# Four modulation rows to a PSUM bank: one copy and one turn where there were four

## What is computed

```
def adaln(cond, mod_w, mod_b):
    return jnp.split(jax.nn.silu(cond) @ mod_w + mod_b, 6, axis=-1)

for l in range(DEPTH):
    sh_a, sc_a, g_a, sh_f, sc_f, g_f = [m[:, None, :] for m in adaln(c, mod_w[l], mod_b[l])]
    csh_a, csc_a, cg_a, csh_f, csc_f, cg_f = adaln(c_ctx, mod_w[l], mod_b[l])
    hx = modulate(rms_norm(x, norm_mix_g[l]), sh_a, sc_a)
    ...
    x = x + g_a * (y_x @ w_out[l])
    x = x + g_f * swiglu(modulate(rms_norm(x, norm_ffn_g[l]), sh_f, sc_f), ffn_w_in[l], ffn_w_out[l])
```

## Time and profile before

| | |
|---|---|
| median of three executions | 2587.45 us (2583.33 to 2587.89) |
| the profiled execution's own time | 2582.74 us |
| its span, first to last instruction | 2581.0 us |
| TensorE matmuls busy | 2403.8 us, 93% of the span |
| VectorE busy | 1536.8 us, 60% |
| ScalarE busy | 1014.6 us, 39% |
| matmuls of the turns (L697) | 192 records, from 20.6 to 657.2 us |
| matmuls of modulation chunks (L714) | 384 records, 51.9 us |
| copies of rows (L1169) | 24, of 573 to 599 ns |
| mean granted TensorE clock | 0.966 of full speed |

### The profile page before, as it was taken

The page is one execution under the profiler, slowest core; times in us unless marked ns, Lnnn a source line. Parts: engine busy times, 40 slices in busy tenths (PEclk is TensorE's granted clock), DMA queues, the critical chain, the costliest instruction groups (busy, mean ns, idle before and its releaser), DMA issues.

```text
span 2581.0 us, 33638 instructions
## 1 busy us (share of the span) xinstructions
PE 2403.8 (93%) x14430; PEld 2063.1 (80%) x14430; DVE 1536.8 (60%) x1957; ACT 1014.6 (39%) x1214; POOL 0.2 (0%) x4
## 2 busy tenths in 40 slices
PE   5978989999989899899899998999998999999997
PEld 3765667777768767899878876899987978779997
DVE  3777553233346566655667668574667657766565
ACT  4245542121233134434554343343465434334344
POOL 0000000000000000000000000000000000000000
PEclk8989999999999999999999999999999999999999
DMA  7440133444323231445445453445544545344552
GB/s 290 165 175 1 52 145 148 184 169 167 114 98 114 72 76 46 151 180 196 167 177 183 147 190 129 163 180 181 183 172 157 190 147 198 126 175 157 187 182 98
DMA packets 61115, 389.22 MB, mean 151 GB/s; under 512 B 6568, under 2 KB 11048, under 8 KB 15784
## 3 DMA queue, kind: packets, MB, share of 16 engines
q1 hardware_dynamic: 60968, 387.08, 41.6%
HBM read 386.00 MB, written 1.05 MB: 150 GB/s over the span
## 4 chain that ended last, share of the span: by engine, by line
PE 76%; DVE 15%; ACT 5%; issue 3%; DMA 1%; SPq 0%; DVEq 0%; ACTq 0%
PE PS L468 22%; PE PS L469 21%; PE PS L470 21%; DVE w_lo L1432 4%; PE PS L641 2%; PE PS L672 2%; PE PS L714 2%; DVE BIG L1939 2%; ACT w_hi L1042 1%; PE PS L654 1%; PE PS L602 1%; PE PS L858 1%; PE PS L840 1%; PE PS L697 1%; ACT xn L1120 1%
## 5 line engine op out<-in xcount | busy, mean ns | idle before, releaser
L1432 DVE TENSOR_TENSOR w_lo<-raw,w_hi 128x2048 fp32r<-128x2048 f32 x300 | 682.6, 2290 | 568.8 <-ACT w_hi L1042 566.5
L1042 ACT ACTIVATE w_hi<-raw 128x2048 fp32r<-128x2048 f32 x300 | 571.4, 1911 | 765.3 <-PE PS L470 468.2
L468 PE MATMUL PS<-x_hi,w_hi 128*128 128x256 f32 (+1 forms) x2048 | 634.2, 310 | 29.1 <-DVE w_lo L1432 12.2
L469 PE MATMUL PS<-x_lo,w_hi 128*128 128x256 f32 (+1 forms) x2048 | 630.2, 308 | 0.0
L470 PE MATMUL PS<-x_hi,w_lo 128*128 128x256 f32 (+1 forms) x2048 | 629.5, 307 | 0.0
L468 PEld LDWEIGHTS PS<-x_hi,w_hi 128*128 128x128 f32 x2048 | 397.5, 194 | 57.3 <-issue 23.1
L469 PEld LDWEIGHTS PS<-x_lo,w_hi 128*128 128x128 f32 x2048 | 397.6, 194 | 16.4
L470 PEld LDWEIGHTS PS<-x_hi,w_lo 128*128 128x128 f32 x2048 | 397.2, 194 | 16.8
L468 PE MATMUL PS<-w_hi,x_hi 128*128 128x512 f32 (+1 forms) x800 | 321.1, 401 | 31.5 <-DVE w_lo L1432 20.0
L469 PE MATMUL PS<-w_lo,x_hi 128*128 128x512 f32 (+1 forms) x800 | 316.9, 396 | 0.0
L470 PE MATMUL PS<-w_hi,x_lo 128*128 128x512 f32 (+1 forms) x800 | 316.5, 396 | 0.0
(11 more groups left out here) (276 smaller groups left out, 2415.0 us busy)
## 6 DMA issues: line engine op xcount, KB each, us to landing
raw<-chunks_in SPq DMA_DIRECT2D x348, 1024.0 KB, 4.8
bias_ring<-brows_in SPq DMA_DIRECT2D x32, 256.0 KB, 5.0
G<-nrows_in SPq DMA_DIRECT2D x2, 1536.0 KB, 6.9
free_b<-rel_in SPq DMA_DIRECT2D x4, 512.0 KB, 8.0
BIG<-rel_in SPq DMA_DIRECT2D x4, 512.0 KB, 10.0
tabt<-tabs_in SPq DMA_DIRECT2D x1, 1536.0 KB, 10.5
X<-x_in SPq DMA_DIRECT2D x1, 1024.0 KB, 8.4
X<-ctx_in SPq DMA_DIRECT2D x1, 1024.0 KB, 10.4
```

The costliest lines, as they stand in the source:

```text
L468: pe.matmul(o, lhs[0], rhs[0], start=start, stop=False, **more)
L469: pe.matmul(o, lhs[0], rhs[1], start=False, stop=False, **more)
L1042: act.activation(w_hi[:, i % HI_RING, :], ring[:, n % RING, :], ACT.Copy).then_inc(*hi_ready.now(n))
L1432: dve.tensor_tensor(w_lo[:, c % RING, :], ring[:, c % RING, :], w_hi[:, i % HI_RING, :].bitcast(F32), ALU.subtract).then_inc(*lo_ready.now(c))
```

## The change

Up to four rows now share a bank. The condition's two columns stand in the middle of a strip of 38 columns (`COND_W`) that is otherwise zero, and row i of a "pack" takes a window of 32 columns such that its two numbers land in lanes 2i and 2i + 1 of each quarter. All chunks of a pack accumulate in one bank, the first clears it, the last ends it. One copy and one turn of four matmuls follow for the pack, with as many columns of a wider `sel_c` as it has lanes (8 or 4); the turn writes, for each quarter of the row, two columns to each row's place in bank 4, 8 columns apart. The rows go in seven packs: (0 to 3), (4 to 7), (10, 11), (8, 9) of layer 0 and (0 to 3), (4 to 7), (8 to 11) of layer 1. The order of layer 0's second part becomes 4, 5, 6, 7, 10, 11. Packs use banks 5 and 6 in turn; bank 7 is no longer one of theirs, and the transposes of the latent projections (`turn_bank`) use banks 4, 5 and 7 where they used 5, 6 and 7. The scalar program copies a pack where it copied the pack's last row, the others' copies are gone. The early part of the tables' transfer is 264 columns where it was 258, and every table behind `sel_c` stands six columns further on. The transfers of weights, the number of modulation chunks and all other work are as before.

```diff
-MOD_PARTS = (((0, 1, 2, 3), (4, 5, 10, 11, 6, 7), (8, 9)), (tuple(range(12)),))
+MOD_PARTS = (((0, 1, 2, 3), (4, 5, 6, 7, 10, 11), (8, 9)), (tuple(range(12)),))
+MOD_PACKS = [(0, (0, 1, 2, 3)), (0, (4, 5, 6, 7)), (0, (10, 11)), (0, (8, 9)),
+             (1, (0, 1, 2, 3)), (1, (4, 5, 6, 7)), (1, (8, 9, 10, 11))]
+PACK = 4
+COND_W = 32 + 2 * (PACK - 1)
...
-MOD_BANKS = 3
-EARLY_TABS = 258
+MOD_BANKS = 2
+EARLY_TABS = 264
...
         def turn_bank(key, b):
-            return 5 + b if key in ("mlac", "mlakr") else 4 + b % 4
+            return (4, 5, 7)[b] if key in ("mlac", "mlakr") else 4 + b % 4
...
-                l, j = state["unturned"]
+                n = state["unturned"]
                 state["unturned"] = None
+                js = MOD_PACKS[n][1]
                 claim(4)
-                pe.wait_ge(*mod_rows.after(l, j))
-                rows = mod_rows_of(l, j)
+                pe.wait_ge(*mod_rows.after(n))
+                rows = mod_rows_of(n)
+                by_row = PS[:, 4, 0:96].rearrange("p (j s c) -> p j s c", s=4, c=2)
+                sel = tab("sel_c")[:, 0:2 * len(js)].rearrange("p (j c) -> p j c", c=2)
                 for s in range(4):
-                    at = 8 * j + 2 * s
-                    mm = pe.matmul(PS[:, 4, at:at + 2], rows[:, s * P:s * P + P], tab("sel_c"), start=True, stop=True)
-                mm.then_inc(*mod_turned.now(l, j))
+                    mm = pe.matmul(by_row[:, js[0]:js[-1] + 1, s, :], rows[:, s * P:s * P + P], sel, start=True, stop=True)
+                mm.then_inc(*mod_turned.now(n))
...
                 b = 5 + n % MOD_BANKS
-                if kg == 0:
+                first = i == 0 and kg == 0
+                if first:
                     mod_turn()
                     claim(b)
                 c, w = take_raw("mod", l)
+                at = 2 * (PACK - 1 - i)
                 for kt in range(4):
-                    mm = pe.matmul(PS[32 * kt:32 * kt + 32, b, :], cond[:, 4 * kg + kt, :], w[:, kt, :],
-                                   start=kg == 0, stop=kg == 1, skip_group_check=True)
-                mm.then_inc(*projected.now("mod", l, j, kg))
+                    mm = pe.matmul(PS[32 * kt:32 * kt + 32, b, :], cond[:, 4 * kg + kt, at:at + 32], w[:, kt, :],
+                                   start=first, stop=i == last and kg == 1, skip_group_check=True)
...
                 split_to(at + 1)
                 n = (at - first - 4) // 2
-                if 1 <= n <= 12:
-                    modulation(1, n - 1)
+                if n in (4, 8, 12):
+                    modulation(3 + n // 4)
                 split_to(at + 2)
...
             for k in range(KD):
                 square(("mix", 0), 4, k)
-            modulation(0, 0)
-            modulation(0, 1)
             first_ev = place_of[plan["first chunk", "ev_in", 0]]
 
             root_mod(("mix", 0), 4)
-            modulation(0, 2)
-            modulation(0, 3)
+            modulation(0)
             split_to(first_ev)
```

More of the change, by code:

```diff
@@ L92, in tables @@
     put("ident", np.eye(P))
-    put("sel_c", np.arange(P)[:, None] % 32 == np.arange(2)[None, :])
+    put("sel_c", np.arange(P)[:, None] % 32 == np.arange(2 * PACK)[None, :])
     tok = np.arange(SEQ)
@@ L298, in build_program @@
         diag = bias_[:, 288:544].rearrange("p (b k) -> p b k", b=2)
-        cond = bias_[:, 544:800].rearrange("p (k c) -> p k c", c=32)
+        cond = bias_[:, 544:544 + KD * COND_W].rearrange("p (k c) -> p k c", c=COND_W)
         yT_na = pair_of((xnr_[:, 0:2048], xnr_[:, 2048:4096]), 256, 8)
@@ L400, in turn_bank, with mod_rows_of @@
         def turn_bank(key, b):
-            return 5 + b if key in ("mlac", "mlakr") else 4 + b % 4
[L403 to L406, removed]
+            return (4, 5, 7)[b] if key in ("mlac", "mlakr") else 4 + b % 4
+        def mod_rows_of(n):
+            return mod_row_bufs[0 if n < 3 else 1][:, (n % 4) * 512:(n % 4) * 512 + 512]
         def gain_of(key, k):
@@ L689, in mod_turn @@
                     return
-                l, j = state["unturned"]
+                n = state["unturned"]
                 state["unturned"] = None
+                js = MOD_PACKS[n][1]
                 claim(4)
-                pe.wait_ge(*mod_rows.after(l, j))
-                rows = mod_rows_of(l, j)
+                pe.wait_ge(*mod_rows.after(n))
+                rows = mod_rows_of(n)
+                by_row = PS[:, 4, 0:96].rearrange("p (j s c) -> p j s c", s=4, c=2)
+                sel = tab("sel_c")[:, 0:2 * len(js)].rearrange("p (j c) -> p j c", c=2)
                 for s in range(4):
-                    at = 8 * j + 2 * s
-                    mm = pe.matmul(PS[:, 4, at:at + 2], rows[:, s * P:s * P + P], tab("sel_c"), start=True, stop=True)
-                mm.then_inc(*mod_turned.now(l, j))
+                    mm = pe.matmul(by_row[:, js[0]:js[-1] + 1, s, :], rows[:, s * P:s * P + P], sel, start=True, stop=True)
+                mm.then_inc(*mod_turned.now(n))
             def mod_chunk():
-                n, kg = divmod(state["m"], 2)
-                if n >= len(MOD_SEQ):
+                seq, kg = divmod(state["m"], 2)
+                if seq >= len(MOD_SEQ):
                     mod_turn()
@@ L706, in mod_chunk @@
                 state["m"] += 1
-                l, j = MOD_SEQ[n]
+                l, j = MOD_SEQ[seq]
+                n = next(n for n, (layer, js) in enumerate(MOD_PACKS) if layer == l and j in js)
+                i, last = MOD_PACKS[n][1].index(j), len(MOD_PACKS[n][1]) - 1
                 b = 5 + n % MOD_BANKS
-                if kg == 0:
+                first = i == 0 and kg == 0
+                if first:
                     mod_turn()
@@ L712, in mod_chunk @@
                 c, w = take_raw("mod", l)
+                at = 2 * (PACK - 1 - i)
                 for kt in range(4):
-                    mm = pe.matmul(PS[32 * kt:32 * kt + 32, b, :], cond[:, 4 * kg + kt, :], w[:, kt, :],
-                                   start=kg == 0, stop=kg == 1, skip_group_check=True)
-                mm.then_inc(*projected.now("mod", l, j, kg))
+                    mm = pe.matmul(PS[32 * kt:32 * kt + 32, b, :], cond[:, 4 * kg + kt, at:at + 32], w[:, kt, :],
+                                   start=first, stop=i == last and kg == 1, skip_group_check=True)
+                if i == last and kg == 1:
+                    mm.then_inc(*projected.now("mod", n))
+                    reader[b] = mod_rows.after(n)
+                    state["unturned"] = n
+                else:
+                    mm.then_inc(*projected.now(("chunk", c)))
                 used(c)
-                if kg == 1:
-                    reader[b] = mod_rows.after(l, j)
-                    state["unturned"] = (l, j)
             def mod_end(l, part):
@@ L1161, in attend, with modulation @@
                         at_unit(u)
-            def modulation(l, j):
-                n = MOD_SEQ.index((l, j))
-                act.wait_ge(*projected.after("mod", l, j, 1))
+            def modulation(n):
+                act.wait_ge(*projected.after("mod", n))
                 if n >= 4:
-                    act.wait_ge(*mod_turned.after(*MOD_SEQ[n - 4]))
-                act.activation(mod_rows_of(l, j), PS[:, 5 + n % MOD_BANKS, :], ACT.Copy).then_inc(*mod_rows.now(l, j))
+                    act.wait_ge(*mod_turned.after(n - 4))
+                act.activation(mod_rows_of(n), PS[:, 5 + n % MOD_BANKS, :], ACT.Copy).then_inc(*mod_rows.now(n))
             def swiglu(l, tiles):
@@ L1199, in _ @@
             act.wait_ge(*const_ready.after())
-            act.activation(cond[:, :, 0:2], col("cond").rearrange("p (k c) -> p k c", c=2),
+            act.activation(cond[:, :, 2 * (PACK - 1):2 * PACK], col("cond").rearrange("p (k c) -> p k c", c=2),
                            ACT.Silu).then_inc(*cond_ready.now())
@@ L1214, in _ @@
             split_to(first_ev + 2)
-            modulation(0, 4)
             root("cq", 4, 256)
@@ L1220, in _ @@
             split_to(first_ev + 4)
-            modulation(0, 5)
             copy_turned("mlac")
@@ L1226, in _ @@
             split_to(first_ev + 6)
-            modulation(0, 10)
             root(("dak", 0), 16, 64)
@@ L1242, in _ @@
                 ins.then_inc(*stored_s.now("ukv", 0, t, 0))
-            modulation(0, 11)
+            modulation(1)
             act.wait_ge(*stored_s.after("ukv", 0, 3, 0))
@@ L1249, in _ @@
             root("mlak", 16, 128)
-            modulation(0, 6)
-            modulation(0, 7)
+            modulation(2)
             split_to(first_ev + 11)
@@ L1274, in _ @@
                     split_to(first + 3)
-                    modulation(0, MOD_PARTS[0][2][0])
                     split_to(first + 4)
-            modulation(0, MOD_PARTS[0][2][1])
+            modulation(3)
             root_mod(("ffn", 0), 4)
@@ L1638, in modulation @@
                 js = sorted(MOD_PARTS[l][part])
-                dve.wait_ge(*mod_turned.after(l, MOD_PARTS[l][part][-1]))
```

(2 more changed lines are left out.)

2 lines of the change are left out of this document (1 added, 1 removed).

## The result

The changed kernel runs in 2561.57 us (median of four, 2558.36 to 2565.35), the kernel before in 2585.45 in the same comparison: a ratio of 0.9908, 95% interval 0.9889 to 0.9927. In a second comparison it is 2563.41 against 2583.84 us, ratio 0.992 (0.9906 to 0.9933). The sign was right, and so were the places where a gain was forecast. The size of one of them, the start, was not, and some microseconds came at places that the forecast had put at nothing.

The account below looks back on a forecast made before the run. TensorE, busy 93% of the span, was taken as the bound, so turns count only where it doesn't wait. 6.3 + 7.0 + 1.6 + 0.3 - 0.2 = 15.0 us off 2585.4 gave 2570.4 us, range 2564 to 2579.

Parts of the forecast that it names:

- FFN: Layer 0's FFN: eight turns of 0.79 us leave TensorE's chain, row 10's gives nothing; 6.3 us gained.
- Rivals 3 and 4: Turns were filler, TensorE waits for `w_lo`: 1.7 us gain, chance 0.06; FFN landings grow, slower: 2592 us, chance 0.04.
- Start: Kernel's start: chunks no longer wait behind turns, `norm_mod` starts at 33.6 to 35.3 us, not 41.92; 7.0 us gained.
- The first rival: Start gives nothing because the chunks' landing sets row 3's end: gain 8.0 us, time 2577.4, chance 0.14.
- Projections: Layer 0's projections: two turns of 0.79 us leave the chain, row 10's and row 6's give nothing; 1.6 us gained.
- The transfer behind them: Last transfer behind layer 0's projections, 7.67 us long: between 0 and 1.5 us of loss, taken as 0.
- Output projection: Layer 0's output projection: one turn goes, but the copy must wait for ScalarE's square; 0.3 us gained.
- Small edits: Moved tables taken as 0, with 1 us either way; turns writing 8 columns for 2 cost 0.2 us.
- The base: Whole kernel before: average of four executions, 2585.4 us, from which gains were subtracted; 2.5 us either way.

Follow-up runs that it names:

- the start alone: Changed kernel with only rows 0 to 3 of layer 0 in one pack, every other row with its own copy and turn: 2572.38 us, ratio 0.9956 to the kernel before.
- second pair of profiles: Repeat profiles without edits, of the kernel before (2585.21 us) and of the changed kernel (2563.41 us).
- single rows: Changed kernel with 24 single-row copies and turns, order and banks as before, keeping only the wider table and strip of 38 columns: 2583.68 us, ratio 0.9997.
- turns last: Changed kernel with rows 0 to 3 single, their four turns all behind the part's last chunk: 2576.62 us against 2584.19, ratio 0.9962.
- the filler in the old start: Kernel before with ten extra unread matmuls of 256 columns ahead of row 0's turn: 2581.64 us against 2584.19, ratio 0.9987.
- second profile of before: Kernel before, no edit, profiled a second time: 2585.21 us, `norm_mod` beginning at 46.05 us.
- with the filler: Changed kernel with extra unread matmuls in TensorE's start waits, six ahead of the third chunk, fourteen behind the turn: 2562.84 us, ratio 0.9918.

## Why the prediction was wrong in size

**FFN: right.** Forecast 6.3 us for eight turns of 0.79, none for row 10's, no stall for `w_lo`. Both pairs of profiles have 6.8 to 6.9, 0.5 to 0.6 of it a shorter last transfer. That the packs shorten it isn't shown: it took 4.72 us in the kernel with the start alone, which has the old turns here. Periods are 23.9 and 24.7 us as said. Rivals 3 and 4 are refuted.

**Start: the mechanism was right, the term was mis-sized, at 7.0 us where 10.8 to 11.5 were measured.** The time for the changed kernel held: `norm_mod` at 34.6 to 34.9 forecast, 34.84 and 35.28 measured. Some of that was luck. On the way through TensorE the sums took 1.81 us for 1.05, so the broadcast ended at 26.3 for 25.4, and the four chunks then took 4.6 us where even the fast end had 5.2. The constants were ready at 33.3, near that end (33.0), where I had put 7.0 near the slow one. What came last was the split, at 34.8, 0.4 us behind the range that I had for it. What failed was the other end of the difference, 41.92 us. I took it from one execution without asking which level of TensorE's clock it had been made at, though the sum itself used both rates from the same rows (3.33 and 1.90 us a pair) and had a spread of 1.7 us for the new kernel. (The 3.33 was itself no slow rate but a mix of both; a slow pair takes 3.61.) The same doubt held for the old one, where three pairs and four turns hang on it: at the slow rate the last pair takes 3.61 for 1.90, and the last two turns 1.87 for 1.05 each. That is 3.3 of the 4.1 us, the rest is a little of every earlier step. So the term is 10.8 us in the second pair of profiles and 11.5 in the timed kernel with the start alone, not 7.0. The first rival (the start gives nothing) is refuted by the same kernel.

**Projections: 1.6 forecast, 1.6 found** (from 7.1 to 8.6 us in the first pair, up to the chunk at 171 us), with row 10's turn worth nothing as said. The transfer behind them gave 1.4 where I took 0 from a range of up to 1.5 us of loss. With packs it took 6.2 to 6.4 us. With a turn between the slots' releases it took 7.5 to 7.7 in five profiles (three of before, single rows, turns last), but only 6.3 and 6.4, from the end of the chunk to the split that waited for it, in two others (the filler in the old start, the start alone), where the same turn stands in the same place. So the turn there doesn't decide it. That the packs brought the 1.4 us isn't shown, and the cause stays open.

**Output projection: right.** 0.3 us was forecast. From the modulation pair to the turn, before and after:

```profile
315.62 1.85 PE PS L714 x16
...
342.86 1.05 PE PS L697 x8
```

```profile
305.34 1.85 PE PS L722 x16
...
332.29 1.03 PE PS L701 x8
```

That is 27.24 and 26.95 us, and 27.24 and 26.97 in the second pair. The attention ahead of it, where nothing was changed, gave 0.2 us in the first pair and 2.0 in the second, with a granted clock of 0.96 in the second profile of before and 0.99 in the changed kernel.

**Small edits: right.** Tables and strip 0 (ratio 0.9997), a turn's wider and broken output 0.

**The base.** Against the second profile of before the terms are 10.8 + 1.6 + 1.3 - 0.2 + 2.0 + 6.9 = 22.4 us by the last turn (1.3 is the transfer behind the projections, 2.0 the stretch from there to the FFN, and -0.2 what the projections lose and gain beside the two turns), and 3 come back later. With the start at 11 in place of 7, and 1.9 for the two transfers, my own sum would have been about 21 us and the forecast 2564.5. The rest to the measured 2561.57 and 2563.41 us is within the scatter.

The range was too narrow for the same reason. It gave the base 2.5 us for scatter of the whole, and nothing for the chance that the profiled start of before was not the usual one.

## What to carry to other kernels

A difference of two times needs both ends checked: before the old kernel's profile serves as the base of a sum, see by the durations of like instructions whether it ran at the usual clock level, above all in a stage with waits, and get a second profile where the level could go either way.

An engine that runs its program in order and meets a wait with landed work behind it loses more by the wait's place than by its length. Here moving the turns behind the chunks gave 10.1 us, and merging four into one 1.1 more.

Work that belongs to a later stage should not stand ahead of the last small step of this one, where the next stage waits for that step.

## What was unexpected of the hardware

The recorded granted clock was 1.00 in one execution and 0.50 in another for a start whose chunk pairs took 3.61 us in both.

Ten idle-time matmuls raised the level for the next steps (a turn 1.05 us for 1.87), and by 24.46 it was low again, though TensorE had worked since 20.65 (the sums 1.87 us). The Trainium skill (TensorE: Matmul & The Clock Gate, "What's actually happening") has the throttled state as the default that activity lifts, and the fast turn agrees; that the changed kernel's gain was given back in a later stretch (2562.84 us with the filler) no run explains.

Four plain float32 matmuls with 128 columns of weights took 0.79 us in the chain with 2 moving columns and with 8, whether these were written side by side or in four pieces.

One and the same transfer of 1 MB took 7.5 to 7.7 us in five profiles with the old turns around it and 6.3 and 6.4 us in two others with them. No run tells why.
